# A long fp32 block on one core: every buffer behind the parameters moved up by 64 bytes, from 64 to 0 modulo 128

## What is computed

```python
def first_block(x, c, ...):                     # two layers
    for l in range(2):
        mod = silu(c) @ w_ada[l] + b_ada[l]     # six vectors of 2048
        h = rms_norm(x, g_pre_mix[l]) * (1 + scale_a) + shift_a
        y = token_mixer(h, w_in[l], ..., w_out[l])   # mLSTM heads and windowed attention
        x = x + gate_a * rms_norm(y, g_post_mix[l])
        h = rms_norm(x, g_pre_mlp[l]) * (1 + scale_m) + shift_m
        x = x + gate_m * rms_norm(square(relu(h @ w_up[l])) @ w_down[l], g_post_mlp[l])

def second_block(x, ...):
    h = s5_layer(x, ...)                        # w_in, state space scan, w_glu, w_out
    k, v, cum = shared_kv(h, ...)               # kv_w
    return fox_layer(h, ..., k, v, cum)         # fox_w_in, attention, fox_w_out
```

## Time and profile before

| what | value |
|---|---|
| runs | 3263.88, 3269.46, 3270.71 us; median 3269.46 us |
| profiled execution | span 3265.3 us from its first to its last instruction; no other time is given for it |
| the span against the median | 4.2 us less |
| TensorE clock granted, mean | 0.980 of full speed |
| instructions | 49414 |
| loaded and stored | 790 MB, 242 GB/s in the mean |

### The profile page before, as it was taken

How to read it: one execution, slowest core, us unless ns; L and a number is a source line. 1 busy time by engine, 2 the same in 40 slices (tenths; PEclk the granted TensorE clock), 3 DMA queues, 4 the chain that set the end, 5 groups by cost and what they waited for, 6 DMA issues and landing times. The chain is left out here.

```text
span 3265.3 us, 49414 instructions
## 1 busy us (share of the span) xinstructions
PE 3117.1 (95%) x20322; PEld 2698.4 (83%) x20322; DVE 2510.6 (77%) x3120; ACT 1569.2 (48%) x2327; POOL 0.2 (0%) x4
## 2 busy tenths in 40 slices
PE   4899999999999999999999999999998999999998
PEld 3788878888888878888888888887886888888887
DVE  7997999798888787777887566788569677556665
ACT  2455654344444556765444444445443455333454
POOL 0000000000000000000000000000000000000000
PEclk7999999999999999999999999999999999999999
DMA  9777859888888645553687666775655554554353
GB/s 409 301 306 302 316 228 353 334 334 339 335 337 328 232 180 194 217 209 129 259 327 263 228 229 206 268 259 207 225 173 181 181 182 142 207 181 146 139 184 112
DMA packets 136976, 790.24 MB, mean 242 GB/s; under 512 B 20081, under 2 KB 38897, under 8 KB 46001
## 3 DMA queue, kind: packets, MB, share of 16 engines
q1 hardware_dynamic: 108002, 754.65, 62.1%
q10 hardware_dynamic: 28752, 32.45, 3.0%
HBM read 769.28 MB, written 17.76 MB: 241 GB/s over the span
## 5 line engine op out<-in xcount | busy, mean ns | idle before, releaser
L1518 DVE TENSOR_TENSOR wl<-raw,wh 128x2048 fp32r<-128x2048 f32 x479 | 1096.4, 2289 | 244.1 <-ACT wh L874 243.4
L394 PE MATMUL bk<-HX,wh 128*128 128x512 f32 x4592 | 1113.2, 395 | 2.9 <-ACT wh L874 1.6
L394 PEld LDWEIGHTS bk<-HX,wh 128*128 128x128 f32 x4592 | 842.4, 188 | 176.7 <-ACT wh L874 2.7
L874 ACT ACTIVATE wh<-raw 128x2048 fp32r<-128x2048 f32 x479 | 913.6, 1908 | 33.5 <-DMA raw<-in_w_in 26.4
L394 PEld LDWEIGHTS bk<-HX,wl 128*128 128x128 f32 x4592 | 571.4, 188 | 29.3 <-DVE wl L1518 6.5
L394 PE MATMUL bk<-HX,wl 128*128 128x256 f32 x4592 | 578.8, 278 | 2.6 <-DVE wl L1518 2.6
L394 PE MATMUL bk<-hb,wh 128*128 128x512 f32 x2048 | 494.1, 393 | 5.5 <-ACT hb L874 5.0
L1526 DVE SCALAR_TENSOR_TENSOR raw<-raw,cb 128x2048 f32<-128x2048 f32 x192 | 437.1, 2283 | 13.9 <-DMA raw<-in_w_ada 13.9
L394 PEld LDWEIGHTS bk<-hb,wh 128*128 128x128 f32 x2048 | 376.6, 188 | 82.2 <-ACT hb L874 5.8
L394 PEld LDWEIGHTS bk<-hb,wl 128*128 128x128 f32 x2048 | 256.4, 189 | 12.3 <-DVE wl L1518 1.8
L394 PE MATMUL bk<-hb,wl 128*128 128x256 f32 x2048 | 258.9, 279 | 0.9 <-DVE wl L1518 0.9
(11 more groups left out here) (276 smaller groups left out, 2690.6 us busy)
## 6 DMA issues: line engine op xcount, KB each, us to landing
raw<-in_w_ada SPq DMA_DIRECT2D x192, 1024.0 KB, 6.1
raw<-in_w_up SPq DMA_DIRECT2D x128, 1024.0 KB, 5.2
raw<-in_w_down SPq DMA_DIRECT2D x128, 1024.0 KB, 5.1
raw<-in_w_in SPq DMA_DIRECT2D x68, 1024.0 KB, 5.1
raw<-in_kv_w SPq DMA_DIRECT2D x33, 1024.0 KB, 4.8
raw<-in_w_out SPq DMA_DIRECT2D x32, 1024.0 KB, 4.8
raw<-in_s_w_in SPq DMA_DIRECT2D x32, 1024.0 KB, 4.9
raw<-in_fox_w_in SPq DMA_DIRECT2D x32, 1024.0 KB, 4.7
```

Source lines behind the costliest of these rows:

```text
L394: return e.matmul(o_, l_, r_, start=start, stop=stop, skip_group_check=True)
L874: return e.activation(o_, i_, f, **kw)
L1518: return e.tensor_tensor(o_, a_, b_, op)
```

## The change

A0 is rounded up to a multiple of 128 where it was taken as it came. It becomes 102144 = 798 x 128, and M with it 134912 = 1054 x 128. Nothing else differs: the instructions, their order on every engine, their shapes, their waits and the loads are the same; each buffer from HX on begins 64 bytes further.

```diff
         PK = at("pk", (16,), o, F32R); o += 64
-        A0 = o
+        A0 = (o + 127) // 128 * 128
         HX = at("HX", (KT, 2, T), A0, F32R)
         M = A0 + 32 * kb
```

## The result

| | before | changed |
|---|---|---|
| median of the runs | 3269.54 us (3263.88 to 3270.71) | 3303.31 us (3300.96 to 3306.49) |
| ratio | | 1.0106, 95% interval 1.0094 to 1.0118 |
| span of the profiled execution | 3265.3 us | 3299.0 us |

The account below looks back on a forecast made before the run. TensorE's own matmul pace was taken to bound the kernel. 150.9 us gained on slabs, less 4.7 where VectorE sets the pace and 2 of waiting, gave 144: 3269.5 - 144 = 3125 us, range 3108 to 3275.

Parts of the forecast that it names:

- the second part's first: Moving operands of the 479 split slabs: 5.18 us a slab, 5.20 kept, from 5.515; gain 150.9 us if all shows.
- straddled fetches: TensorE's moving reads: 128-byte fetches crossing 128-byte borders cost one extra half-clock step each; chance 0.50, time 3125 us.
- a pause in the reader: TensorE's moving reads: the reader pauses once in every 128 bytes wherever they lie, so slabs stay at 5.515 us.
- rival 1: The loss sits in TensorE's reader itself, wherever bytes begin; the time stays at 3269 us (3263 to 3276); chance 0.38.
- Weight loads: ... Nothing: TensorE's weight loads: 190 ns with raw at a multiple of 128, 189 with qf at 64, so costed at nothing.
- The forecast's other sum of 0: SBUF lines of 16 bytes and no larger ones: 64 and 128 are both multiples, so the change does nothing.
- Rival 2: Weight and moving reads collide at equal offset modulo 128: 3.3 ns a matmul, 51 us, time 3320 us; chance 0.08.
- The argument against it: Plain matmuls: kf and qf both at 64 modulo 128, hf and raw apart, yet they take 380 and 379 ns.
- What else was costed at nothing: VectorE and ScalarE buffer moves (bound 5 ns either side) and DMA into rampw (bound 1 us): no gain or loss.
- The signs that were named: MLP stretches: two slabs in 10.4 us if right, still 11.03 for the pause, more than that for the conflict.

Follow-up runs that it names:

- e2_all64: Against the changed kernel, every buffer moved 64 bytes further, so weights are at 64 and moving operands at 0 modulo 128; 3269.7 us.
- e4_w64: Against the changed kernel, 64 bytes put in before WH alone, so WH and WL are at 64 and moving operands at 0 modulo 128; 3268.8 us.

## Why the prediction was wrong

- **The step that failed** is the second part's first: "if the straddle is the cause, a slab takes 16 x 0.216 + 16 x 0.108 = 5.18 us". The loss of 1/16 was read correctly, and so was that it goes with bytes and not with instructions. The two explanations of it, straddled fetches and a pause in the reader, were both left standing by the trace, and the forecast took the first. The runs with moving operands at 0 modulo 128 (e2_all64, e4_w64) keep the loss whole, at 3270 and 3269 us. The loss belongs to the reading of 4 new bytes for each column, rival 1's premise, and it gives the change nothing to gain: the slab forecast at 5.20 us would have stayed at 5.515.
- **The second step that failed** is the line "Weight loads: ... Nothing", which put the term at nothing that then decided the sign. The loads do take as long as before (188 ns with HX and wh in both kernels); what the duration of a load can't show is what it costs the matmul beside it. With the distance moved from 64 to 128 that is 105 ns a slab: a slab took 5.62 us, and the 305 slabs together 32.1 us more. The forecast's other sum of 0, from the 16-byte lines of the Trainium skill ("SBUF — State Buffer", Door 1), failed as well: that no larger unit counts was the forecast's addition to the page, and 64 bytes cost 34 us.
- **Rival 1's time** was wrong too, because it assumed that nothing else depends on addresses.
- **Rival 2** named what happened: weight reads and moving reads cost each other time by their distance. Its size for a matmul was close, 3.3 ns against 3.7 for 512 columns (me,wa at 233.0 ns, mc,wa at 229.3) and 3.1 for 256 (118.6 and 115.5). That the size came out so near is in part luck, since the cost isn't the fixed step for each 128 bytes that it was worked out from. Its total of 51 us was too large because it charged all 7664 pairs; the 305 slabs that run at bare pace paid 32.1 of the 34. Its mechanism was only half right: the unit is 256 and not 128, the same offset is not the worst case, and the cost depends on the pair. It got a chance of 0.08 and lay outside the range. The argument against it, that kf with qf and hf with raw take 380 and 379 ns, came from plain float32 matmuls, which have half their read time free, as the text itself noted; such rows can't speak against a conflict at full rate.
- **What else was costed at nothing** stayed at nothing: VectorE's operations (X<-X,tmp 1225 ns and tmp<-yu,rsy 1219, against the earlier trace rows), plain matmuls, the wait for rampw (40.5 us, against 40.1 in the earlier trace rows).
- **The signs that were named** did their work: 16 matmuls with wh at 3.71 to 3.73 us and more than 11.03 us for two slabs meant the conflict.

Still open: what makes 256 the unit and 64 the good distance, and how one stream's pace comes to depend on the one before. The runs give the table and not its inner cause. Layouts in which the distance changes from chunk to chunk were not tried.

## What to carry to other kernels

When a stream is bound by TensorE itself and reads 4-byte elements at full clock, the distance between the weights and the moving operand, modulo 256 bytes, was worth up to 2.8% of a slab here in steps of 32 (5673 against 5517 ns), and 4% at the worst distance tried, 4 bytes; measure it on streams of the same order and shape, both kinds together, since single streams don't add. A round address is no improvement in itself: the kernel before had the best of the distances tried by accident, and 64 bytes of a small buffer in between were part of it. Two causes that leave the same mark in a trace should get a small kernel of streams before they get a forecast of 144 us.

## What was not expected of the hardware

- TensorE read a moving fp32r operand at about 16/17 of its full pace even at the best distance: 229 ns for 512 columns against 216 for bf16 or for one element repeated.
- Weight loads slow such a stream down by up to 156 ns in 5517 (the worst pair of 64), by distance alone, and by 233 at a distance of 4 bytes. With 32 weight columns distance 128 costs nothing over 64.
- Equal streams settle into a repeating pattern that depends on the stream before: 113.7 ns for 256 columns at distance 192 after a long stream at 192, and 117.9 after one at 0.
